# The product of token block 0 straight out of the bank on VectorE, and a head's exponentials ahead of another head's copy

## What is computed

```python
x = x + 0.5 * swiglu(rms_norm(x, norm), w_gate, w_up, w_down)

def swiglu(h, w_gate, w_up, w_down):          # w_gate, w_up: 1024 x 2816, w_down: 2816 x 1024
    return (jax.nn.silu(h @ w_gate) * (h @ w_up)) @ w_down
```

```python
s = jnp.einsum('bhqd,bhkd->bhqk', q_blk, k) * scale + (c_blk[..., :, None] - c[:, :, None, :])
p = jax.nn.softmax(jnp.where(kpos[None, :] <= qpos[:, None], s, -jnp.inf), axis=-1)
```

## Time and profile before

| | |
|---|---|
| median of 3 runs | 2299.2 us |
| the profiled execution's own time | 2299.22 us |
| its span, first to last instruction | 2297.4 us |
| TensorE matmul busy | 2286.0 us (100%) |
| TensorE weight load busy (beside the matmuls) | 1921.1 us (84%) |
| VectorE busy | 1812.6 us (79%) |
| ScalarE busy | 1381.5 us (60%) |
| GpSimd busy | 26.4 us (1%) |

### The profile page before, as it was taken

One profiled execution on the slowest core, in us unless ns is written; L12 is line 12 of the kernel. 1 busy time (PEld: TensorE's weight loads), 2 busy tenths in 40 slices (PEclk: granted clock), 3 DMA queues, 4 the chain that ended last, 5 costly groups with the idle time before them and its releaser, 6 DMA issues.

```text
span 2297.4 us, 33084 instructions
## 1 busy us (share of the span) xinstructions
PE 2286.0 (100%) x12395; PEld 1921.1 (84%) x12395; DVE 1812.6 (79%) x1974; ACT 1381.5 (60%) x1513; POOL 26.4 (1%) x32
## 2 busy tenths in 40 slices
PE   9999999999999999999999999999999999999999
PEld 7888889888888898888888888888888888888887
DVE  8887867788898877768889886577888888467987
ACT  6657466565566566556657555656565655564655
POOL 0000010000000000000000000000000000000000
PEclk9999999999999999999999999999999999999999
DMA  7666444566565554546556656546655665545653
GB/s 256 214 213 184 150 149 155 171 204 201 176 213 188 192 177 146 176 136 216 183 196 202 220 186 208 163 153 205 198 186 185 208 200 193 184 165 165 210 184 128
DMA packets 331063, 427.25 MB, mean 186 GB/s; under 512 B 17544, under 2 KB 296208, under 8 KB 330960
## 3 DMA queue, kind: packets, MB, share of 16 engines
q1 hardware_dynamic: 324832, 412.73, 55.0%
q10 hardware_dynamic: 4976, 9.52, 1.2%
q0 software_dynamic: 1152, 3.55, 0.5%
HBM read 424.69 MB, written 1.05 MB: 185 GB/s over the span
## 4 chain that ended last, share of the span: by engine, by line
PE 99%; DVE 1%; ACT 0%; issue 0%; ACTq 0%; DVEq 0%
PE ps L1371 15%; PE ps L1124 13%; PE ps L1126 13%; PE ps L1125 13%; PE ps L1236 13%; PE ps L1241 13%; PE ps L1237 13%; PE ps L1351 2%; PE ps L1137 1%; PE ps L1487 0%; PE ps L1556 0%; PE ps L1566 0%; DVE arena L2355 0%; PE ps L1718 0%; PE ps L1653 0%
## 5 line engine op out<-in xcount | busy, mean ns | idle before, releaser
L1859 DVE TENSOR_TENSOR wlo<-raw,whi 128x2048 fp32r<-128x2048 f32 x318 | 721.1, 2285 | 145.5 <-ACT whi L571 144.4
L571 ACT ACTIVATE whi<-raw 128x2048 fp32r<-128x2048 f32 x312 | 592.9, 1902 | 233.0 <-PE ps L1126 185.6
L1236 PE MATMUL ps<-whi,hT 128*128 128x512 f32 x1280 | 500.0, 391 | 0.0
L1237 PE MATMUL ps<-whi,hT 128*128 128x512 f32 x1280 | 498.4, 389 | 0.0
L1124 PE MATMUL ps<-whi,hT 128*128 128x512 f32 x856 | 342.8, 401 | 0.2
L1241 PE MATMUL ps<-wlo,hT 128*128 128x512 f32 x1280 | 342.4, 389 | 0.3 <-DVE wlo L1859 0.3
L1126 PE MATMUL ps<-whi,hT 128*128 128x512 f32 x856 | 334.2, 390 | 0.0
L1125 PE MATMUL ps<-wlo,hT 128*128 128x512 f32 x856 | 333.8, 390 | 0.0
L1236 PEld LDWEIGHTS ps<-whi,hT 128*128 128x128 f32 x1280 | 240.3, 188 | 53.1 <-ACT arena L688 2.8
L1241 PEld LDWEIGHTS ps<-wlo,hT 128*128 128x128 f32 x1280 | 239.6, 188 | 51.3 <-DVE wlo L1859 2.0
L1237 PEld LDWEIGHTS ps<-whi,hT 128*128 128x128 f32 x1280 | 240.3, 188 | 50.0
(11 more groups left out here) (336 smaller groups left out, 3049.9 us busy)
## 6 DMA issues: line engine op xcount, KB each, us to landing
raw<-in_w_ffn SPq DMA_DIRECT2D x264, 512.0 KB, 4.5
raw<-in_w_in SPq DMA_DIRECT2D x144, 512.0 KB, 4.8
raw<-in_ffn_w_down SPq DMA_DIRECT2D x88, 512.0 KB, 4.2
raw<-in_ffn_w_up SPq DMA_DIRECT2D x86, 512.0 KB, 4.1
raw<-in_ffn_w_gate SPq DMA_DIRECT2D x86, 512.0 KB, 5.4
raw<-in_w_out SPq DMA_DIRECT2D x32, 512.0 KB, 4.3
gain<-in_gains ACTq DMA_DIRECT2D x16, 512.0 KB
raw<-in_cross_wk SPq DMA_DIRECT2D x16, 512.0 KB, 4.1
```

Of the source, the lines that this page charges most:

```text
L571: act.activation(whi[:, s, :, 0:cols], raw[:, s, :, 0:cols], ACT.Copy).then_inc(hi_ready, units)
L1236: pe.matmul(ps[:, bank, :], hT_hi[:, t, k0 + k, :], whi[:, s, k, :], start=first and k == 0, stop=False, skip_group_check=True)
L1237: pe.matmul(ps[:, bank, :], hT_lo[:, t, k0 + k, :], whi[:, s, k, :], start=False, stop=False, skip_group_check=True)
L1859: dve.tensor_tensor(wlo[:, s, :, 0:cols], raw[:, s, :, 0:cols], whi[:, s, :, 0:cols].bitcast(F32), ALU.subtract).then_inc(lo_ready, units)
```

## The change

It has two parts.

- In each feed-forward network ScalarE's scaled copy of the up columns of token block 0 (L678) is left out, and with it the semaphore `up_out` and ScalarE's wait on `half_inverse`. `kept_product` is replaced by `bank_product` with a token block as argument: VectorE multiplies the up columns of bank G (in step 1 of bank TR + 1), scaled by hinv, with the silu. TensorE's wait ahead of `gate_up(stp, 1)` is now on `prod_ready`, on the first product of this step. VectorE's order isn't changed.
- In ScalarE's list of the first block's mixer `fox_exp(6)` stands ahead of `fox_pT(5)`.

```diff
                 def first_evac(stp, c=0, bank=G):
                     act.wait_ge(first_half, WIDE * f + stp + c)
                     act.activation(silu_g[:, 0, :], ps[:, bank, 0:256], ACT.Silu, scale=stat[:, 0, 2, 0:1]).then_inc(silu_done, 1)
-                    act.activation(prod[:, 0, :], ps[:, bank, 256:512], ACT.Copy, scale=hinv[:, 0:1]).then_inc(up_out, 1)
...
-                act.wait_ge(half_inverse, f + 1)
                 first_evac(1, bank=TR + 1)
...
                 fox_pT(4)
+                fox_exp(6)
                 fox_pT(5)
-                fox_exp(6)
                 fox_exp(7)
...
-                    pe.wait_ge(up_out, WIDE * f + stp + c)
+                    pe.wait_ge(prod_ready, PRODS * f + TB * (stp + c) + 1)
                     gate_up(stp, 1, c)
...
-                pe.wait_ge(up_out, WIDE * (f + 1))
+                pe.wait_ge(prod_ready, PRODS * f + TB * last + 1)
                 gate_up(last, 1)
...
-                def kept_product(stp, c=0):
-                    dve.wait_ge(up_out, WIDE * f + stp + c)
-                    dve.tensor_tensor(prod[:, 0, :], prod[:, 0, :], silu_g[:, 0, :], ALU.mult).then_inc(prod_ready, 1)
-
-                def bank_product(stp, c=0):
-                    dve.wait_ge(silu_done, PRODS * f + TB * (stp + c) + 2)
-                    dve.scalar_tensor_tensor(out=prod[:, 1, :], in0=ps[:, G, 256:512], scalar=hinv[:, 1:2], in1=silu_g[:, 1, :],
+                def bank_product(stp, t, c=0, bank=G):
+                    dve.wait_ge(silu_done, PRODS * f + TB * (stp + c) + t + 1)
+                    dve.scalar_tensor_tensor(out=prod[:, t, :], in0=ps[:, bank, 256:512], scalar=hinv[:, t:t + 1], in1=silu_g[:, t, :],
                                              op0=ALU.mult, op1=ALU.mult).then_inc(prod_ready, 1)
...
                     block_sums(stp - 1, c)
-                    kept_product(stp, c)
+                    bank_product(stp, 0, c)
                     block_lo(1, stp - 1, c)
                     parts_lo(stp - 1, c)
                     block_lo(2, stp - 1, c)
-                    bank_product(stp, c)
+                    bank_product(stp, 1, c)
```

More of the change, by code:

```diff
@@ L299, in build @@
         silu_done = sem("silu_done")
-        first_half, up_out, half_inverse, parts_out, parts_summed = (
-            sem(n) for n in ("first_half", "up_out", "half_inverse", "parts_out", "parts_summed"))
+        first_half, half_inverse, parts_out, parts_summed = (sem(n) for n in ("first_half", "half_inverse", "parts_out", "parts_summed"))
         block_summed, block_hi_ready, block_lo_ready, block_used = (sem(f"block_{n}") for n in ("summed", "hi_ready", "lo_ready", "used"))
@@ L2065, in ffn @@
                 block_sums(0, between=lambda: parts_lo(0))
-                kept_product(1)
-                bank_product(1)
+                bank_product(1, 0, bank=TR + 1)
+                bank_product(1, 1)
                 block_lo(1, 0)
@@ L2088, in ffn @@
                 split_lo(b, l, d)
-                kept_product(last)
+                bank_product(last, 0)
                 wait_unit(dve, b, l, d - 3)
@@ L2097, in ffn @@
                     flush(7 + m, *x)
-                bank_product(last)
+                bank_product(last, 1)
                 split_lo(b, l, off + FFN_UNITS - 1)
```

## The result

| | before | after |
|---|---|---|
| median | 2299.59 us (5 runs, 2299.05 to 2302.53) | 2394.84 us (5 runs, 2391.55 to 2402.72) |
| ratio to before, 95% interval | | 1.0418 [1.0407, 1.043] |
| the profiled execution (span) | 2299.22 (2297.4) us | 2398.47 (2396.7) us |
| granted TensorE clock, mean | 1.000 | 0.993 |

The changed kernel is slower by 95 us. The forecast was 2388.7 us with a range of 2370 to 2412.

A forecast was written before the change was run, and what follows sets the result against it. TensorE was taken to bound the kernel, so added waits are paid in full: 2299.2 us + 93.4 for feed-forward stalls − 3.9 for the attention reorder = 2388.7 us, with an 8-in-10 range of 2370 to 2412.

The forecast's parts named there:

- What bounds the kernel: TensorE, busy 2286.0 of 2297.4 us; work taken off ScalarE or VectorE gains nothing, waits added to TensorE are paid fully.
- (a): Feed-forward: dropping ScalarE's copy (37.5 us of ScalarE) and its half_inverse wait gains 0; VectorE loses a 0.2 us wait.
- (b): Feed-forward product: reading the bank instead of SBUF takes 484 instead of 418 ns, 0.066 us more per product.
- (c), the closed loop: Feed-forward steps 3 to 9: TensorE waits for VectorE's queued product, 0.83 us each; loop 16.96 us against 16.12.
- (c), steps 2 and 10: Feed-forward stalls: 3.11 us in step 2; in step 10, 2.43 us in six calls, 3.56 and 3.87 in two.
- (d): First block's attention, twice: exponentials of head 6 ahead of head 5's copy remove TensorE's idle time, gaining 3.9 us.
- the better end: Head 6's norm waits for one GpSimd multiplication, not two: gain 1.95 us per layer instead of 1.3.
- Rival (3), the clock: TensorE's clock falls in 16 new pauses of 2.4 to 3.9 us, costing 46 us: 2435 us; chance 10%.
- signs of being wrong: Profile after: a steady step of 16.12 us, a granted clock under 1.00, or a product starting before the block sums end.
- the clock's 0 in the sum: The sum 2299.2 + 93.4 − 3.9 us counted no time for falls of TensorE's clock.
- (1): Rival: no stall, VectorE reaches the first product in time, only the attention gain stays: 2295.3 us; chance 4%.
- (2): Rival: VectorE's operations close up in steady steps, the 0.83 us vanishes, only head and tail stalls stay: 2342.2 us; 8%.

The follow-up runs named there:

- version ahead of all sums: Changed kernel with the first product moved in VectorE's order ahead of all three block sums, in step 10 ahead of the split: 2303.61 us.
- products alone: Changed kernel with the old order of head 6's exponentials and head 5's copy put back: 2398.19 us.
- only TensorE's wait moved: Kernel before, ScalarE's copy and the old SBUF product kept, with TensorE's wait moved from the copy to the product: 2392.86 us.
- product ahead of the third sum: Changed kernel with the first product ahead of only the third block sum in steps 2 to 9, step 10 as changed: 2355.90 us.
- product behind block_lo(1): Changed kernel with the first product one operation later on VectorE, after block_lo(1), in steps 2 to 9: 2554.22 us.
- step 2's pause filled: Changed kernel with 13 added matmuls into an unused bank during step 2's pause in each network: 2389.97 us.
- attention part alone: Kernel before with only the exponentials of head 6 moved ahead of head 5's copy: 2295.86 us.
- version in steady steps only: Changed kernel, but steps 2 and 10 keep ScalarE's copy and the wait on it; only steps 3 to 9 as changed: 2337.34 us.

## Why the prediction was right

- **What bounds the kernel:** right. ScalarE lost 24.9 us of work and VectorE's work hardly changed (1812.6 to 1817.4), and only TensorE's waits and, at them, its clock moved the time.
- **(a), (b), the forms:** right. The form costs 0.07 us where it lies on the path (16.87 against 16.80). VectorE's wait of 0.19 us behind the product is gone, as (a) has it, and only its idle piece grew by it: 2.12 + 0.75 + 0.19 = 3.06, measured 3.07, where I had 2.95.
- **(c), the closed loop:** right as a mechanism, in both directions of the dose. The waits were forecast at 93.4 us and came to 95.7 − 72 × 0.04 = 92.8 us. What a wait costs was mis-sized: I priced the step at 16.96 us and it is 16.87, since 0.09 us come back at each restart. Over 72 waits that is 6.5 us too much.
- **(c), steps 2 and 10:** the waits are right to 0.02 us (3.14, 2.46, 3.59 and 3.89, with the 0.04 between any two loads in them, against 3.11, 2.43, 3.56 and 3.87).
- **(d):** right. One of GpSimd's multiplications stands in the norm's way, not two, and the norm is ready in time: 3.7 us forecast as 3.9. The Trainium skill (SBUF — State Buffer, the single rule on the shared port pair) has the pair held for a whole instruction while the other waits. The trace agrees with this much: one scaling took 2.55 us and ended 0.08 us behind the multiplication's end at 322.17. The rule gives the pair to the one that starts first, and here the rows don't bear it out: they have the scaling start at 319.71 and the multiplication at 319.75, and the scaling waited. GpSimd's times are rough in this profile, so which of them was first stays open; I had taken the norm's start in the gap as a reason for the better end.
- **Rival (3), the clock:** half right, and wrongly set apart from the forecast. A granted clock under 1.00 was one of my signs of being wrong, and it came: 0.993. I gave it 10% and 16 falls at 2.9 us; ten of the 16 long pauses met a fall, at 1.6 us each, so 16 us. The term that was mis-sized is the clock's 0 in the sum. The longest pause of the old trace (2.00 us, the matmuls' own 1.77) had shown no fall; I called longer ones unknown and still put them at nothing. The Trainium skill (TensorE: Matmul & The Clock Gate, Part 1) says that idle time lets the clock fall, and the trace agrees: 0.50 from 47.56 to 50.97.
- **Rivals (1) and (2):** fell. Every steady step is 16.87 us long and has its wait, 56 of the 72, so VectorE didn't reach its product in time, and the stall didn't close up. (1)'s condition, a product that starts 0.84 us earlier, was made by hand in the version ahead of all sums, and its time came to 2303.6.

The mechanism was right, but that the forecast of 2388.7 is only 6 us below the median is partly luck. The restart's −6.5 and the clock's +16.1 have opposite signs, and each is larger than the 6 us. With both, the sum is near 2398, the time of the profiled execution with its ten falls (2398.47); the median run has fewer falls.

## What to carry to other kernels

When a buffer's release moves from one engine to another, what counts isn't how long the new releasing operation takes, but when its turn comes in its engine's queue: a product that takes 0.48 us cost 0.75 us a step because 10 us of work stood ahead of it and began only after TensorE's last signal. Close the loop on paper (TensorE's signal, the queue up to the release, TensorE's restart) and compare it with the step; and ask in the same look where in its queue the operation could stand, since one place higher, ahead of the last sum, a steady step was back at 16.13 us. Idle time on the releasing engine isn't room by itself: here it lay behind the release, where it could only grow.

## What the runs showed of the hardware

- Pauses of TensorE's matmuls between 1.7 and 3.9 us were met by a fall of its granted clock to 0.50 in some cases and not in others, and pauses of one length differ from execution to execution. In the profiled executions:
  - changed kernel: 8 of 8 pauses of 2.7 us, 2 of 6 of 2.0 us, neither of the two of 3.2 and 3.5 us;
  - products alone: 6 of 8 of 2.7 us, none of 6 of 2.0 us, both of 3.2 and 3.5 us, none of 2 of 1.8 us;
  - only TensorE's wait moved: 5 of 8 of 2.6 us, none of 6 of 2.0 us, 3.1 us yes and 3.4 us no, 1 of 2 of 1.8 us;
  - product ahead of the third sum: 10 of 14 of 2.0 us, both of 3.2 and 3.5 us;
  - product behind block_lo(1): 36 of 56 of 1.8 us and all 16 that are longer;
  - step 2's pause filled: 2 of 6 of 2.0 us, both of 3.2 and 3.5 us;
  - kernel before: none of 2 of 1.8 us; attention part alone: one of 1.7 us near its start.

  Pauses of 0.4 to 0.5 us: none of 56, in each of five kernels. That the pause is what brings the fall is shown by filling it (0 of 8 for 8 of 8 in step 2). What decides between pauses of one length is open; no run was made for it.
- Each fall costs 1.55 to 1.6 us here, and their number differs from run to run. The changed kernel's spread goes with it: 2391.55 us at a mean clock of 0.995, 2402.72 us at 0.990; the version in steady steps only, with no fall in its profile, spreads over 0.6 us.
- A wait costs TensorE 0.09 us less than the time that its weight load is held back (steps of 16.95, 16.86 and 16.04 us in the version with steady steps alone).
